# Query and key norms of a decoder layer on one Trainium2 core: sums of squares by turned tiles, ScalarE and VectorE in place of products with ones

## The reference, cut to what matters

```python
def rms_norm(x, w):
    y = xf * lax.rsqrt(jnp.mean(xf * xf, axis=-1, keepdims=True) + EPS)
    return (y * w.astype(F32)).astype(x.dtype)

def l2norm(x):
    return (xf * lax.rsqrt(jnp.sum(xf * xf, axis=-1, keepdims=True) + EPS)).astype(x.dtype)
...
    qkv, dn_buf = causal_conv(dn_qkv, dn_buf0, lw['dn_conv_w'])
    qkv = jax.nn.silu(qkv)
    q = l2norm(q.reshape(bn, s, DN_HEADS, DN_DK)) * (DN_DK ** -0.5)
    k = l2norm(k.reshape(bn, s, DN_HEADS, DN_DK))
...
    fq = rms_norm(fq.reshape(bn, s, FOX_HEADS, FOX_HD), lw['fox_qn_w'])
...
    mq = rms_norm(mq.reshape(bn, s, MEM_HEADS, MEM_HD), lw['mem_qn_w'])
```

## Time and profile before

| | us |
|---|---|
| median of 3 runs | 1677.81 |
| lowest, highest | 1675.85, 1680.12 |
| span of the profiled execution (first to last instruction) | 1673.4 |
| PE busy | 1622.7 (97%) |
| DVE busy | 862.9 (52%) |
| ACT busy | 535.1 (32%) |
| POOL busy | 507.4 (30%) |

### The profile page before, as it was taken

The page is one execution under the profiler, slowest core; times in us unless marked ns, Lnnn a source line. Parts: engine busy times, 40 slices in busy tenths (PEclk is TensorE's granted clock), DMA queues, the critical chain, the costliest instruction groups (busy, mean ns, idle before and its releaser), DMA issues. The chain is left out here.

```text
span 1673.4 us, 26271 instructions
## 1 busy us (share of the span) xinstructions
PE 1622.7 (97%) x10707; PEld 1551.8 (93%) x10707; DVE 862.9 (52%) x1256; ACT 535.1 (32%) x918; POOL 507.4 (30%) x379
## 2 busy tenths in 40 slices
PE   5999999999999999999999999999999999999999
PEld 4989989999999999999889989999989999889976
DVE  4657653344444442790287772444668551895611
ACT  6322243222222222233334442311145222654200
POOL 1424415343343312811254551222212221103400
PEclk9999999999999999999999999999999999999999
DMA  4212155222222114542276353135210332534521
GB/s 156 53 26 51 34 155 134 71 70 70 70 71 70 52 51 130 160 119 63 88 196 191 108 175 108 46 120 164 58 38 27 103 100 60 153 123 152 149 79 58
DMA packets 189364, 163.17 MB, mean 98 GB/s; under 512 B 18380, under 2 KB 157055, under 8 KB 188726
## 3 DMA queue, kind: packets, MB, share of 16 engines
q1 hardware_dynamic: 189246, 161.51, 33.4%
HBM read 131.38 MB, written 30.22 MB: 97 GB/s over the span
## 5 line engine op out<-in xcount | busy, mean ns | idle before, releaser
L276 POOL TENSOR_TENSOR wL<-w_raw,wH 128x1024 fp32r<-128x1024 f32 (+1 forms) x112 | 241.5, 2156 | 802.9 <-ACT wH L269 802.7
L335 PE MATMUL ps<-hH,wH 128*128 128x344 f32 x1920 | 457.0, 340 | 12.4 <-PEq L196 3.6
L335 PE MATMUL ps<-hL,wH 128*128 128x344 f32 x1920 | 418.7, 320 | 0.0
L335 PE MATMUL ps<-hH,wL 128*128 128x344 f32 x1920 | 417.8, 320 | 0.0
L335 PEld LDWEIGHTS ps<-hH,wH 128*128 128x128 f32 x1920 | 314.5, 189 | 26.2 <-issue 10.1
L335 PEld LDWEIGHTS ps<-hL,wH 128*128 128x128 f32 x1920 | 325.9, 189 | 0.2
L335 PEld LDWEIGHTS ps<-hH,wL 128*128 128x128 f32 x1920 | 323.5, 188 | 0.0
L269 ACT ACTIVATE wH<-w_raw 128x1024 fp32r<-128x1024 f32 (+1 forms) x116 | 108.5, 935 | 116.3 <-PE ps L335 107.4
L2891 POOL TENSOR_SCALAR fa_logits<-fox_c_bc,token_scalars 128x128 f32<-128x128 f32 (+7 forms) x32 | 59.9, 1872 | 55.1 <-PE ps L2916 35.7
L1846 ACT ACTIVATE d_m<-ps 128x512 f32<-128x512 f32 x48 | 28.7, 598 | 134.8 <-PE ps L2028 134.8
L1235 DVE SCALAR_TENSOR_TENSOR m_th<-m_th,ps 128x1032 f32<-128x1032 f32 x24 | 29.5, 1228 | 61.7 <-PE ps L335 56.7
(11 more groups left out here) (576 smaller groups left out, 2773.6 us busy)
## 6 DMA issues: line engine op xcount, KB each, us to landing
w_raw<-in_w_in SPq DMA_DIRECT2D x80, 512.0 KB, 5.1
m_th<-gate_spill SPq DMA_DIRECT2D x28, 516.0 KB, 4.5
gate_spill<-d_gate SPq DMA_DIRECT2D x18, 516.0 KB, 3.0
fa_kv<-in_cache_fox_k SPq DMA_DIRECT2D x32, 256.0 KB, 3.0
fa_kv<-in_cache_fox_v SPq DMA_DIRECT2D x32, 256.0 KB, 3.5
w_raw<-in_w_branch SPq DMA_DIRECT2D x32, 256.0 KB, 2.8
gate_spill<-fa_gate SPq DMA_DIRECT2D x10, 516.0 KB
x_rows<-in_x_prompt SPq DMA_DIRECT2D x8, 512.0 KB, 6.5
```

The source lines that it names most:

```text
L276: pool.tensor_tensor(self.wL[:, t % 2, 0:nk], self.raw_at(t)[:, 0:nk], self.wH[:, t % 2, 0:nk].bitcast(F32), ALU.subtract).then_inc(self.w ...
L335: last = pe.matmul(self.ps[:, b + g, 0:cols], w[:, t % 2, k], x[:, k, g * cols:(g + 1) * cols], start=(k == 0 and n == 0), stop=(k == nk - ...
```

## The change

The product with ones is gone in all three places. In its place, half a tile (four blocks of 128 tokens, a *group*) is turned by four PE transposes into one PSUM bank (6 in the convolution stage, 7 in the query stages); ACT squares the bank's 512 columns into SBUF; DVE sums each row over the 128 channels, which now lie along the free dimension, four sums for each instruction. There are two groups for each tile, 32 in all, numbered x. The next group's transposes wait until the one before is squared (one bank), and ACT's squaring of group x waits until DVE has summed group x-2 (two buffers). ACT's old squaring of the tile in SBUF goes.

```diff
+class SquareSums:
+    def pe(self, pe, x):
+        j, half = x // 2, x % 2
+        if x:
+            pe.wait_ge(self.squared, x)
+        for y in range(H):
+            t = H * half + y
+            last = pe.transpose(self.K.ps[:, self.bank, y * P:(y + 1) * P], self.src(j)[:, t * P:(t + 1) * P],
+                                self.K.ident[:])
+        last.then_inc(self.turned, 1)
+    def act(self, act, x):
+        act.wait_ge(self.turned, x + 1)
+        if x >= 2:
+            act.wait_ge(self.summed, x - 1)
+        act.activation(self.T[:, x % 2], self.K.ps[:, self.bank], ACT.Square).then_inc(self.squared, 1)
+    def dve(self, dve, x):
+        dve.wait_ge(self.squared, x + 1)
+        dve.tensor_reduce(self.SUM[:, H * x:H * x + H], heads(self.T[:, x % 2]), AX.X, ALU.add
+                          ).then_inc(self.summed, 1)
...
 conv_tiles, ACT, ahead of the evacuation of tile j (behind split_hi):
+                        if 3 <= j < squares + 3:
+                            norms.act(act, 2 * (j - 3))
+                            norms.act(act, 2 * (j - 3) + 1)
...
-                    if 2 <= j < squares + 2:
-                        act.wait_ge(fin, j - 1)
-                        if j >= 4:
-                            act.wait_ge(sums, j - 3)
-                        act.activation(SQ[:, j % 2], OUT(j - 2)[:, 0:SEQ], ACT.Square).then_inc(sq, 1)
 conv_tiles, DVE, ahead of the convolution of tile j (behind dve_values):
+                    if 3 <= j < squares + 3:
+                        norms.dve(dve, 2 * (j - 3))
+                        norms.dve(dve, 2 * (j - 3) + 1)
 conv_tiles, PE:
-                    if 3 <= j < squares + 3:
-                        pe.wait_ge(sq, j - 2)
-                        for t in range(TT8):
-                            x = (j - 3) * TT8 + t
-                            last = pe.matmul(K.ps[:, 6, x:x + 1], SQ[:, (j - 1) % 2, t * P:(t + 1) * P], K.ones[:],
-                                             start=True, stop=True)
-                        last.then_inc(sums, 1)
+                    def meanwhile(k, j=j):
+                        if 3 <= j < squares + 3 and k in (0, 3):
+                            if k == 0:
+                                pe.wait_ge(fin, j - 2)
+                            norms.pe(pe, 2 * (j - 3) + k // 3)
...
 project_tiles, ACT, behind the turns and ahead of the evacuation of tile j; the last pair behind the last tile:
+                    if RQ is not None and j >= 1:
+                        norms.act(act, 2 * j - 2)
+                        norms.act(act, 2 * j - 1)
 project_tiles, PE:
-                        if RQ is not None and j >= 1 and k >= 2:
-                            norms(pe, j - 1, range((k - 2) * TT8 // 6, (k - 1) * TT8 // 6))
+                        if RQ is not None and j >= 1 and k in (4, 6):
+                            if k == 4:
+                                pe.wait_ge(*K.emptied(t0 + j - 1))
+                            norms.pe(pe, 2 * (j - 1) + (k - 4) // 2)
 project_tiles, DVE:
-                    dve.wait_ge(sums, H)
-                    v.do(dve.tensor_scalar(flat(QS), K.ps[:, 7, 0:H * TT8], 1.0 / P, EPS, ALU.mult, ALU.add))
+                    for x in range(2 * n):
+                        norms.dve(dve, x)
+                    dve.wait_ge(norms.summed, 2 * n)
+                    v.do(dve.tensor_scalar(flat(QS), flat(QS), 1.0 / P, EPS, ALU.mult, ALU.add))
...
 attend, PE, in the lead:
-                    if 1 <= x <= NORMS:
-                        last_norms(pe, x - 1, NORMS)
+                    if x in (1, 2):
+                        if x == 1:
+                            pe.wait_ge(*K.emptied(t0 - 1))
+                        last_norms(pe, x - 1)
```

More of the change, by code:

```diff
@@ L762, in pe_step, with __init__, conv_tiles @@
             pe.wait_ge(self.N["out"], 1)
-def conv_tiles(K, t0, n, name, states, par, silu, OUT, tag, tail, masks=None, squares=0, small=False, side=None,
+class SquareSums:
+    def __init__(self, K, sb, tag, src, SUM, bank):
+        self.K, self.src, self.SUM, self.bank = K, src, SUM, bank
+        self.T = sb(tag + "_squares", [P, 2, H * P])
+        self.turned, self.squared, self.summed = (K.sem(tag + x) for x in ("_sq_turned", "_squared", "_sq_summed"))
+    def pe(self, pe, x):
[16 more added lines that the diff above has]
+                          ).then_inc(self.summed, 1)
+def conv_tiles(K, t0, n, name, states, par, silu, OUT, tag, tail, masks=None, squares=0, sums=None, small=False, side=None,
                first_tiles=None):
@@ L783, in conv_tiles @@
         TH = sb("_th", [P, 2, TOK]) if silu else None
-        SQ = sb("_sq", [P, 2, SEQ]) if squares else None
+        norms = SquareSums(K, sb, tag, OUT, sums, 6) if squares else None
         padded, th, fin = (K.sem(tag + x) for x in ("_padded", "_tanh", "_silu"))
-        sq, sums = K.sem(tag + "_sq"), K.sem(tag + "_sums")
         def tap(j, t):
@@ L920, in left @@
             if squares:
-                eng.wait_ge(sums, squares)
+                eng.wait_ge(norms.summed, 2 * squares)
             if n > 4:
@@ L1491, with __init__ @@
     N_SUMS = 2 * H * TT8
-    def __init__(self, K, kept, c):
+    def __init__(self, K, kept, c, sums):
         nc = K.nc
         n = self.N_SUMS
+        self.sums = sums
         self.K = K
@@ L1530, in dve_first @@
         half = self.N_SUMS // 2
-        dve.tensor_scalar(self.SS[:], K.ps[:, 6, 0:self.N_SUMS], EPS, None, ALU.add).then_inc(N["read"], 1)
+        dve.tensor_scalar(self.SS[:], self.sums[:], EPS, None, ALU.add).then_inc(N["read"], 1)
         dve.wait_ge(N["read"], 1)
@@ L2492, in project_tiles @@
         flat = lambda x_: x_[:].rearrange("p a h -> p (a h)")
-        def norms(pe, j, part):
-            if part.start == 0:
-                pe.wait_ge(sq, j + 1)
-            for t in part:
-                q = j * TT8 + t
-                last = pe.matmul(K.ps[:, 7, q:q + 1], SQ[:, j % 2, t * P:(t + 1) * P], K.ones[:],
-                                 start=True, stop=True)
-            if part.stop == TT8:
-                last.then_inc(sums, 1)
         if True:
@@ L2569, in _ @@
                                        bias=K.bias[:, row + j:row + j + 1]).then_inc(K.evac_act, 1)
-                    if RQ is not None:
-                        act.wait_ge(*K.emptied(t))
-                        if j >= 2:
-                            act.wait_ge(sums, j - 1)
-                        act.activation(SQ[:, j % 2], DST[:, j, 0:SEQ], ACT.Square).then_inc(sq, 1)
                 if ahead:
@@ L2580, in _ @@
                     turns.act(act, turn)
+                if RQ is not None:
+                    norms.act(act, 2 * n - 2)
+                    norms.act(act, 2 * n - 1)
             @block.tensor
@@ L2657, in project_tiles @@
         if RQ is not None:
[L2658 removed]
+            K.last_norms = lambda pe, x: norms.pe(pe, 2 * (n - 1) + x)
 class GateBulk:
@@ L3316, in build @@
                 held = sb("u_rn", [P, 2, H, TT8]), sb("u_gc", [P, 3, H, P])
+                sums = sb("ca_sums", [P, 2 * H * TT8])
                 with ExitStack() as c2:
@@ L3320, in build @@
                                lambda j: K.OT[:, j] if j < H else K.merged[:, j - H], "ca", tail,
-                               masks=masks, squares=2 * H, small=True, first_tiles=K.first_tiles)
-                    units = UnitsAndMemory(K, held, c2, tail, at["mem_kv"])
+                               masks=masks, squares=2 * H, sums=sums, small=True, first_tiles=K.first_tiles)
+                    units = UnitsAndMemory(K, held, c2, tail, at["mem_kv"], sums)
                     KV = units.KV
```

15 lines of the change are left out of this document (7 added, 8 removed).

## The result

| | median us | range, runs | against the kernel before |
|---|---|---|---|
| before, beside it | 1676.76 | 1675.47 to 1680.12, 9 | |
| changed kernel | 1668.78 | 1667.35 to 1674.62, 9 | ratio 0.9959, 95% 0.9948 to 0.997 |
| changed kernel, timed again later | 1666.56 | 1663.66 to 1674.98, 6 | ratio 0.9941, 95% 0.9922 to 0.9961 |

The change makes the kernel faster, by 8.0 us in the first comparison and 11.6 in the second (1678.19 before), where 15.1 were forecast. The profiled execution has a span of 1668.0 us against 1673.4. A timed run lies 1.7 us above its own span (1669.67 against 1668.0), so of the 4.4 us that the forecast carried over only 1.7 belong to the launch; for the rest the profiled execution of before was a quick one.

The account below looks back on a forecast made before the run. PE's queue, busy 97% of the span, was taken as the bound. Convolution stage 4.9, fq and lead 4.9, mq and lead 5.3 make 15.1 us off 1673.4: 1658.3, plus 4.4 carried over: 1662.7 us, range 1658 to 1670.

Parts of the forecast that it names:

- the 4.4 us that the forecast carried over: Whole kernel: the median of the runs lies 4.4 us above the profiled span, added to 1658.3 to give 1662.7.
- Bound and gross gain: PE's queue sets the time; ones cost 28.6 us of PE, transposes 14.1, so 14.5 us gross.
- Rival 4, the clock: All 32 groups: transposes cost PE its full clock, 1711 us; chance 0.05 together with any other loss.
- `pe_sums`: Convolution stage, tile 6: PE arrives before the chain of small columns has ended and waits 1.5 us.
- Tile 8: Convolution stage: squarings stand behind the rounding of tile 9's late weights, so PE waits 0.9 us for the second group.
- Stages fq and mq: Query stages without their leads: tiles give 2.6 us in fq and, to the end of tile 3, 2.7 in mq.
- The two leads: Starts of attentions fa and ma: PE work and factors come earlier, giving 2.3 us in fa and 2.6 in ma.
- Just in time: Lead of fa: factors are ready at +11.1 us, PE needs them at +11.3, so the wait for them goes.
- The stages between pass a shift on: Stages between the changed places: loads and stores follow PE's progress, so no gain is lost there, 0 us.
- the prediction's own sign (the shift at 830 us found again at 1360): Between the lead of fa and stage mq: the forecast would be wrong if the shift at 830 us weren't found at 1360.
- rival 3: An attention or the merges, where DVE or a DMA ends last: the shift is lost, perhaps 3 us stay, 1675; chance 0.06.
- Rival 1: Handovers inside tiles take more: convolution stage gives 2.5 us, leads 1 each, gain 9 us, 1669 us; chance 0.17.

Follow-up runs that it names:

- e8: Changed kernel, rounding ahead of last squarings in query stages, first squaring ahead of rounding in convolution stage, small sums and rows one step later: 1659.7 us, ratio 0.9884.
- e1: Changed kernel with ScalarE's rounding of the attention's second weight tile ahead of the last two squarings in stages fq and mq: 1663.24 us, ratio 0.9906.
- e5: The changed kernel as it is, profiled once more: one run of 1670.24 us, span 1668.5.
- e9: Kernel before with only the convolution stage changed, query stages as before: 1671.56 us, ratio 0.9969.
- e13: The changed kernel as it is, timed a second time and profiled again: 1666.56 us, ratio 0.9941.
- e12: e8 with the load of tile 9's weights also ahead of the small stores: 1660.46 us, ratio 0.9901.
- e14: Changed kernel with tile 9's weight load ahead of the small stores and the rounding ahead of the last squarings in the query stages: 1661.88 us, ratio 0.9905.
- e15: Kernel before with only the convolution stage changed, and tile 9's weight load ahead of the small stores: 1671.68 us, ratio 0.9966.
- e4: Changed kernel with each group's four transposes issued twice, 128 more on PE: 1677.0 us, ratio 1.0001.
- the parts alone: Kernel before with only the convolution stage changed (1671.56 us, 5.8 under its own before), and with only the query stages and leads changed (1669.29 us, 8.1 under).
- e2: Changed kernel with the first squaring of a tile's pair ahead of the rounding of the next weights in the convolution stage: 1665.78 us, ratio 0.9937.
- e6: The kernel before, unaltered, profiled once more: span 1677.2 us.

## Why the prediction was right in direction and too large

By its own steps:

- **Bound and gross gain: right.** A tile gives 0.9 us where nothing waits (in the changed kernel the shift is +1.96 at the evacuation of 170.23 and +1.03 at the next). A group of four is followed by the next step after 0.36 us at the full clock. Rival 4, the clock, falls: from 67 to 197 us the one half-clock stretch stands behind the long stall, none behind a group, and two of the three profiles have none there at all (granted clock 0.99, 1.00 and 1.00 over that stretch).
- **`pe_sums`: right**, 1.3 us against 1.5 forecast. The move in e8 takes it away.
- **Tile 8: right place, wrong bound.** I let rounding end at about 149.0, because the stores start earlier. They didn't (129.99 against 129.72), they took 10.10 us on SyncE in place of 3.68, the load was issued 2.1 us later than before (140.87), and rounding ended at 151.5. The slow stores aren't what sets the long stall apart, though: they took 9.6 to 10.0 us in e1, e5, e9 and e13 too. What differs is the time from the load's issue to the rounding, 7.5 us (e9) to 9.6 (the long one); e1 issued the load later still, at 141.42, and rounded at 149.28. Why it differs no run shows. Of the five profiles with this code at tile 8, four lie near my 0.9 us (0.30 to 1.35); the first cost 2.65 and some 1.7 of half clock on top. I had doubled both waits for my lower end (2.5 us); 1.2 is below it. The forecast had one number where the chip has a spread.
- **Stages fq and mq: right**, 2.64 against 2.6 and 2.90 against 2.7, the 0.46 for the last pair of ones behind the evacuation wait among it.
- **The two leads: the step that failed.** 4.9 us forecast, 0.85 measured, 4.6 with the rounding back in its place (e1). The path to the factors was wrong. I had written that what is pushed back is ScalarE's rounding and GpSimd's split, to +11, and asked only whether PE wants it by then. I never asked what runs beside the split at its new place: VectorE's chain of factors, from +8.2 to +11.1, on which the whole gain of the lead rested. The prediction's "Just in time" took 2.9 us for that chain, as in before, where nothing ran beside it; with the shift held it took 4.96 (819.71 to 824.67). And the price stood in the trace of before. VectorE's timeline, with the split beside it, has the same instruction on 8 columns at 2.36 and at 0.23 us:

```profile
71.81 2.77 POOL L276 TENSOR_TENSOR wL<-w_raw,wH 128x1024 fp32r<-128x1024 f32 x1 [4.91 <-ACT wH L269]
...
72.25 2.36 DVE L886 SCALAR_TENSOR_TENSOR branch_in<-dn_conv_states,half_par,branch_in 128x8 f32<-128x8 f32 x1
...
75.84 0.23 DVE L886 SCALAR_TENSOR_TENSOR branch_in<-dn_conv_states,half_par,branch_in 128x8 f32<-128x8 f32 x1
```

It does so in each tile of the stage whose split falls there. The reductions of the change, beside a split from 151.63 to 154.00, took their 0.69 us:

```profile
152.00 0.69 DVE L793 TENSOR_REDUCE ca_sums<-caca_squares 128x4 f32<-128x512 f32 x1 [1.05 <-ACT caca_squares L789]
```

  The Trainium skill, SBUF — State Buffer, section Who interferes with whom, says this in advance: VectorE and GpSimd share a pair of ports as an exclusive lock, which VectorE wants for an instruction with two inputs in SBUF or for one in a two-port fast mode, and on this chip never for a reduction. The rows agree for two inputs (2.22 and 2.36 us) and for the reduction (0.69); the int32 shift has one input, and whether it runs in such a mode no row shows.
- **"The stages between pass a shift on": wrong in one place**, and by the prediction's own sign (the shift at 830 us found again at 1360) in a second, the half clock in fa, which is before's too. The decode rows of branch A and the keys, from 665.75 to 768.14, take back 0.8 to 3.5 us in all 11 profiles that come there earlier than the first of before (in e12 3.46, in e14 2.94), and 0.03 to 0.86 in the five others. The largest of these are half clock in part: e12, e14, e13 and e15 (3.46, 2.94, 2.85 and 2.47 us) have such a stretch in the stage, behind a wait of PE of 1.8 to 2.6 us, some 1.7 us each (granted clock 0.57 from 748 to 752 in e12, 0.57 and 0.59 from 696 to 700 in e14 and e15, e13's rows above); the other seven have none and lose 0.80 to 2.14. VectorE's chain there starts when the state rows land, and it holds up PE through `wL` (L285) and `e_or`. Before and after, SyncE's issue and VectorE's first instruction:

```profile
657.52 3.99 SPq L2178 DMA_DIRECT2D e_state<-in_state_dn  x4
...
665.12 0.69 DVE L2217 TENSOR_TENSOR e_prod<-e_state,e_row 128x512 f32<-128x512 f32 x1 [22.11 <-DMA e_state<-in_state_dn]
```

```profile
656.61 4.51 SPq L2212 DMA_DIRECT2D e_state<-in_state_dn  x4
...
665.60 0.69 DVE L2251 TENSOR_TENSOR e_prod<-e_state,e_row 128x512 f32<-128x512 f32 x1 [23.48 <-DMA e_state<-in_state_dn]
```

  From issue to use it was 7.6 to 8.0 us in the six profiles that weren't early, 8.7 to 9.5 in the eleven that were. **Why this load takes longer stays open**: e4 has the changed code and isn't early, and has 7.9, so it isn't the code; but nothing was found that keeps its own time there. This is rival 3, to which I gave 0.06, with 0.8 to 3.5 us in place of its 12 and beside the others.

With what was measured the sum is 15.1 - 4.1 (leads) - 1.8 (decode rows, mean of three) - 0.7 (convolution stage with the short stall) = 8.5 us, or 5.5 with the long stall. The 1.4 us of the collision in ma, which the forecast didn't have, come on top: 9.9 or 6.9, against 8.0 and 11.6 timed. Rival 1 had the place (the lead, no slack) and nearly the size, with another cause; its own terms add up to 2.5 + 3.6 + 3.7 = 9.8 us, not 9. And it doesn't quite close: the parts alone give 5.8 + 8.1 = 13.9 us, or 12.5 with the collision counted once, both together 8.0 and 11.6. The decode rows and half clocks after waits may be paid only once too, but the difference between the two timings of the same kernel is as large as what would have to be explained, and I don't claim to have done it.

## What to carry to other kernels

When an instruction is moved on one engine, follow what it releases to the end: the rounding moved 5 us on ScalarE and cost nothing there or on PE, but its GpSimd part landed on VectorE's critical chain and cost 2 us each time. Before pricing such a chain, look in the trace for the same small instruction at two durations; the long one tells what it can't stand beside. And where a stall depends on a load behind stores on one queue, give a range from several executions, since one profile shows one draw.

## What the runs showed of the hardware that I had not expected

- Many VectorE instructions that start while GpSimd's two-input split of 128x1024 runs get nowhere until the split ends. Small ones last just to its end: 2.27 us for 32 int32 columns, 2.22 for a Newton step, 2.36 for 8 columns. A large one does its own work behind it: a product of 128x1024, 1.21 us alone, took 3.18. Not held were an instruction under way when the split started (0.19), a reduction (0.69), a reciprocal of one column (0.15 at 1459.16 of before) and a scaling of 256 columns out of PSUM (0.48 at 1432.20 of before).
- The hold gives as well as takes, and it goes both ways. In both profiles of before a product in ma was held by such a split, and PE waited 1.40 us for what came of it. In the changed kernel, and in e9, where that stage has the old code, the split starts just behind the product (by 0.07 and 0.08 us) and not 0.28 us ahead of it. The product takes its 1.21 us, the split 3.38 in place of 2.38, and 1.4 us are gained that no edit accounts for. Before, and the changed kernel:

```profile
1458.95 2.38 POOL L276 TENSOR_TENSOR wL<-w_raw,wH 128x1024 fp32r<-128x1024 f32 x1 [24.54 <-ACT wH L269]
...
1459.23 3.18 DVE L3062 TENSOR_TENSOR ma_kv<-ma_kv,ma_d_logits 128x1024 f32<-128x1024 f32 x1
```

```profile
1454.85 1.21 DVE L3091 TENSOR_TENSOR ma_kv<-ma_kv,ma_d_logits 128x1024 f32<-128x1024 f32 x1
...
1454.92 3.38 POOL L276 TENSOR_TENSOR wL<-w_raw,wH 128x1024 fp32r<-128x1024 f32 x1 [24.50 <-ACT wH L269]
```

- Eight tiny stores took SyncE 3.68 or 3.69 us in the five profiles with the old convolution stage and in e4; in the other eleven, all with the changed stage, they took 3.97 (e8), 4.64 (e12), 7.00 (e2) or 9.56 to 10.17. These are the same eleven that come early to the decode rows. Why isn't known.
- The half clock behind a wait of PE of about 2 us comes in some executions and not in others of the same code (fa: e6 yes, first profile of before no), at some 1.6 us each; waits of 1.35 us and less in tile 8 never brought it.
